# Attention of a hybrid encoder block on TensorE: score pairs in two row halves, V stationary with normalised probabilities moving in two column halves

## The reference

```python
h = rms_norm(x, mix_norm[l])
z = h @ w_in[l]                       # 1024 -> 2048: q | k | v | p, 512 columns each
a = neighborhood_attention(q, k, v, rpb[l])   # 8 heads of 64
m = multiscale_pool(p, w_pool[l], pool_scale[l])
x = x + jnp.concatenate([a, m], axis=-1) @ w_out[l]

# attention: tokens are a 4 x 64 grid, every query sees all 4 rows and 16 columns around its own
scores = q_r * Dh**-0.5 @ k_r.T + bias        # bias from rpb, by distance of rows and columns
scores = where(col_mask, scores, NEG_INF)
out    = softmax(scores) @ v_r

# pooling, group g of 128 channels, window w = 2, 4, 8, 16
mean = (csum[hi] - csum[lo]) / (hi - lo)      # lo = t - w//2, hi = lo + w, clipped
y    = (mean - p) @ w_pool[g] * scale
```

## Time and profile before

| | |
|---|---|
| median of 3 runs | 987.61 us (985.65 to 989.18) |
| span of the profiled execution | 983.4 us |
| TensorE busy | 958.7 us, 97% |
| VectorE busy | 552.3 us, 56% |
| ScalarE busy | 499.5 us, 51% |
| mean DMA rate | 178 GB/s |

### The profile page before, as it was taken

The page is one execution under the profiler, slowest core; times in us unless marked ns, Lnnn a source line. Parts: engine busy times, 40 slices in busy tenths (PEclk is TensorE's granted clock), DMA queues, the critical chain, the costliest instruction groups (busy, mean ns, idle before and its releaser), DMA issues.

```text
span 983.4 us, 13937 instructions
## 1 busy us (share of the span) xinstructions
PE 958.7 (97%) x4390; PEld 780.2 (79%) x4390; DVE 552.3 (56%) x865; ACT 499.5 (51%) x812; POOL 45.1 (5%) x86
## 2 busy tenths in 40 slices
PE   5989999999999999999989999999999999999996
PEld 4878888877788888888878888888868888888885
DVE  4556555467545665554466556564665565465644
ACT  4555455455625654544375545454664365454542
POOL 0550000010001000000010000000100010000000
PEclk9999999999999999999999999999999999999999
DMA  8998646527223746465367555644542266556441
GB/s 285 234 244 284 211 171 212 173 87 250 93 86 129 244 147 210 167 213 171 129 208 254 193 191 171 209 160 143 171 172 86 86 209 199 190 170 213 145 156 43
DMA packets 123269, 174.75 MB, mean 178 GB/s; under 512 B 8240, under 2 KB 99552, under 8 KB 122976
## 3 DMA queue, kind: packets, MB, share of 16 engines
q1 hardware_dynamic: 117328, 165.17, 50.1%
q0 software_dynamic: 2848, 6.38, 3.0%
q10 hardware_dynamic: 3056, 2.75, 0.8%
HBM read 173.14 MB, written 4.19 MB: 180 GB/s over the span
## 4 chain that ended last, share of the span: by engine, by line
issue 92%; POOL 4%; DMA 2%; PE 1%; ACT 0%; ACTq 0%; DVE 0%; POOLq 0%; DVEq 0%; SPq 0%
POOL bias_scratch L364 3%; POOL rstd L337 1%; DMA bias_scratch<-in_rpb_dram 1%; DMA w_raw<-in_ffn_w_up_dram 1%; POOL mean_eps L334 0%; PE ps L868 0%; POOL rstd_scaled L340 0%; PE ps L869 0%; ACT w_hi L416 0%; PE ps L918 0%; ACT L416 0%; POOL bias L371 0%; DVE normed L850 0%; DVEq L95 0%; ACT xt_hi L431 0%
## 5 line engine op out<-in xcount | busy, mean ns | idle before, releaser
L631 DVE SCALAR_TENSOR_TENSOR w_lo<-w_raw,gain,w_hi 128x512 fp32r<-128x512 f32 x416 | 285.4, 746 | 104.3 <-ACT w_hi L416 103.7
L860 PE MATMUL ps<-w_hi,xt_hi 128*128 128x512 f32 x848 | 338.3, 399 | 2.9 <-DVE w_lo L631 2.8
L861 PE MATMUL ps<-w_lo,xt_hi 128*128 128x512 f32 x848 | 330.4, 390 | 0.0
L863 PE MATMUL ps<-w_hi,xt_lo 128*128 128x512 f32 x848 | 326.2, 391 | 0.0
L416 ACT ACTIVATE w_hi<-w_raw,gain 128x512 fp32r<-128x512 f32 x416 | 265.7, 713 | 99.7 <-PE ps L863 78.2
L623 DVE TENSOR_TENSOR w_lo<-w_raw,w_hi 128x1024 fp32r<-128x1024 f32 x104 | 122.7, 1222 | 121.2 <-ACT w_hi L410 121.1
L860 PEld LDWEIGHTS ps<-w_hi,xt_hi 128*128 128x128 f32 x848 | 159.3, 188 | 39.1 <-DVE w_lo L631 4.7
L863 PEld LDWEIGHTS ps<-w_hi,xt_lo 128*128 128x128 f32 x848 | 159.2, 188 | 34.2
L861 PEld LDWEIGHTS ps<-w_lo,xt_hi 128*128 128x128 f32 x848 | 159.6, 188 | 30.4
L410 ACT ACTIVATE w_hi<-w_raw 128x1024 fp32r<-128x1024 f32 x104 | 104.4, 1052 | 105.0 <-PE ps L863 104.3
L860 PE MATMUL ps<-w_hi,gt_hi 128*128 128x512 f32 x352 | 140.0, 398 | 0.0
(11 more groups left out here) (82 smaller groups left out, 468.3 us busy)
## 6 DMA issues: line engine op xcount, KB each, us to landing
w_raw<-in_ffn_w_gate_dram SPq DMA_DIRECT2D x88, 512.0 KB, 4.0
w_raw<-in_ffn_w_up_dram SPq DMA_DIRECT2D x88, 512.0 KB, 5.1
w_raw<-in_ffn_w_down_dram SPq DMA_DIRECT2D x88, 512.0 KB, 4.0
w_raw<-in_w_in_dram SPq DMA_DIRECT2D x32, 512.0 KB, 4.7
w_raw<-in_w_out_dram SPq DMA_DIRECT2D x16, 512.0 KB, 5.2
bias_scratch<-in_rpb_dram POOLq DMA_DIRECT2D x32, 96.0 KB, 6.7
bias<-bias_scratch POOLq DMA_DIRECT2D x2, 1536.0 KB, 8.0
pool_m<-in_pool_matrix_dram ACTq DMA_DIRECT2D x1, 1024.0 KB, 6.5
```

Source lines behind the costliest of these rows:

```text
L631: nc.vector.scalar_tensor_tensor(w_lo[slot][:, part], w_raw[slot][:, part], g, w_hi[slot][:, part].bitcast(F32), ALU.mult, ALU.subtract).t ...
L860: nc.tensor.matmul(o, hi, wh, start=start, stop=False)
L861: nc.tensor.matmul(o, hi, wl, start=False, stop=False)
L863: last = nc.tensor.matmul(o, lo, wh, start=False, stop=stop)
```

## The change

- **Scores**: `pair_scores` takes two heads at once and alternates between them, the even head in rows 0 to 63 of the array, the odd one in rows 64 to 127. It waits until both heads of the pair before have been read. The places in `after` are thinned out to four pairs.
- **Normalisation**: VectorE's new `normalise` divides the probabilities of a head by their row sum before they are transposed: one reciprocal of two values, two multiplies of 128x256. `transpose_probs` waits for `normalised_ready` and no longer for `probs_ready`. The multiply of the outputs by the inverse sum is gone, and so is the reciprocal of all sums.
- **V times probabilities**: `pair_v` makes V stationary (128 rows x 64 columns) and moves the 256 columns of the transposed probabilities. The even head's output goes to PSUM partitions 0 to 63, the odd head's to 64 to 127. The result comes out with channels on partitions, so the transposes of the outputs are gone, and ScalarE and VectorE make `xt_hi` and `xt_lo` straight from banks 0 and 1.
- **Pool differences**: for the second tile of tokens (k = 1) only the columns from 120 (`POOL_FROM`) on are computed, as the window reaches no further back than 8 tokens. The others are zero in the matrix.
- **Order**: VectorE's queue has the eight `normalise` between its other pieces, and the output projection takes its first half for both row tiles in one go.

```diff
-            def head_scores(layer, h):
-                if h >= 2:
-                    pe.wait_ge(biased_ready, layer * N_HEADS + (h - 1))
-                rows = slice((h % 2) * HEAD_DIM, (h % 2 + 1) * HEAD_DIM)
-                for t in range(TT):
-                    last = nc.tensor.matmul(ps[:, 4 + h % 2, t * SEQ:(t + 1) * SEQ],
-                                            q_t[rows, h // 2, t, :], k_t[rows, h // 2, :, :],
-                                            start=True, stop=True)
-                last.then_inc(scores_ready, 1)
+            def pair_scores(layer, pair):
+                if pair >= 1:
+                    pe.wait_ge(biased_ready, layer * N_HEADS + 2 * pair)
+                for t in range(TT):
+                    for e in range(2):
+                        rows = slice(e * HEAD_DIM, (e + 1) * HEAD_DIM)
+                        last = nc.tensor.matmul(ps[:, 4 + e, t * SEQ:(t + 1) * SEQ],
+                                                q_t[rows, pair, t, :], k_t[rows, pair, :, :],
+                                                start=True, stop=True)
+                        if t == TT - 1:
+                            last.then_inc(scores_ready, 1)
...
             def transpose_probs(layer, h):
-                pe.wait_ge(probs_ready, layer * N_HEADS + (h + 1))
+                pe.wait_ge(normalised_ready, layer * N_HEADS + (h + 1))
...
-            def probs_v(layer, h):
-                wait_probs_t_stored(layer, h)
-                for t in range(TT):
-                    for k in range(TT):
+            def pair_v(layer, pair):
+                wait_probs_t_stored(layer, 2 * pair)
+                wait_probs_t_stored(layer, 2 * pair + 1)
+                cols = slice((pair % 2) * SEQ, (pair % 2 + 1) * SEQ)
+                for k in range(TT):
+                    for e in range(2):
+                        h = 2 * pair + e
                         last = nc.tensor.matmul(
-                            ps[:, t, h * HEAD_DIM:(h + 1) * HEAD_DIM],
-                            scores[:, h, k, t * P:(t + 1) * P],
+                            ps[e * HEAD_DIM:(e + 1) * HEAD_DIM, pair // 2, cols],
                             z[:, k, 3, h * HEAD_DIM:(h + 1) * HEAD_DIM],
+                            scores[:, h, k, :],
                             start=(k == 0), stop=(k == TT - 1))
                 last.then_inc(pv_ready, 1)
...
                     for k in range(TT):
+                        first = POOL_FROM * k
                         last = nc.tensor.matmul(
-                            ps[:, 4 + j, (g % 2) * SEQ:(g % 2 + 1) * SEQ],
-                            z[:, k, 2, g * P:(g + 1) * P], pool_m[:, k, g, :],
+                            ps[:, 4 + j, (g % 2) * SEQ + first:(g % 2 + 1) * SEQ],
+                            z[:, k, 2, g * P:(g + 1) * P], pool_m[:, k, g, first:],
                             start=(k == 0), stop=(k == TT - 1))
...
-                project_z(layer, 2, 1, after={1: lambda: s(1), 3: lambda: s(2),
-                                              5: lambda: (s(3), t(0)), 7: lambda: (s(4), t(1))})
-                project_z(layer, 3, 0, after={1: lambda: (s(5), t(2)), 3: lambda: (s(6), t(3)),
-                                              5: lambda: (s(7), t(4)), 7: lambda: t(5)})
+                project_z(layer, 2, 1, after={3: lambda: s(1), 5: lambda: t(0),
+                                              7: lambda: (s(2), t(1))})
+                project_z(layer, 3, 0, after={1: lambda: t(2), 3: lambda: (s(3), t(3)),
+                                              5: lambda: t(4), 7: lambda: t(5)})
...
+            def normalise(layer, h):
+                dve.wait_ge(probs_ready, layer * N_HEADS + (h + 1))
+                nc.vector.reciprocal(inv_sum[:, h, :], row_sum[:, h, :]).then_inc(inv_ready, 1)
+                dve.wait_ge(inv_ready, layer * N_HEADS + (h + 1))
+                for t in range(TT):
+                    done = nc.vector.tensor_scalar(scores[:, h, t, :], scores[:, h, t, :],
+                                                   inv_sum[:, h, t:t + 1], None, ALU.mult)
+                done.then_inc(normalised_ready, 1)
...
                 add_bias(layer, 1)
                 mix_unit(layer, 7, halves=(0,))
+                normalise(layer, 0)
+                normalise(layer, 1)
                 add_bias(layer, 2)
+                add_bias(layer, 3)
                 mix_unit(layer, 7, halves=(1,))
-                add_bias(layer, 3)
+                normalise(layer, 2)
+                store_probs_t(layer, 1)
                 add_bias(layer, 4)
-                store_probs_t(layer, 1)
+                normalise(layer, 3)
                 add_bias(layer, 5)
                 mix_unit(layer, 8)
+                normalise(layer, 4)
+                store_probs_t(layer, 3)
+                normalise(layer, 5)
                 add_bias(layer, 6)
-                store_probs_t(layer, 3)
                 add_bias(layer, 7)
                 store_kv(layer, 3, 0)
+                normalise(layer, 6)
                 store_probs_t(layer, 5)
+                normalise(layer, 7)
                 store_diffs(layer, 0)
```

More of the change, by code:

```diff
@@ L35 @@
 N_GROUPS = len(POOL_WINDOWS)
+POOL_FROM = 128 - max(POOL_WINDOWS) // 2
 D_FF = 2816
@@ L211, in trunk @@
         inv_ready = sem("inv_ready")
[L212 to L213 removed]
+        normalised_ready = sem("normalised_ready")
         heads_t_hi_ready = sem("heads_t_hi_ready")
@@ L529, in exps @@
                         scores[:, h, t, :], scores[:, h, t, :], ACT.Exp,
-                        bias=neg_max[:, h, t:t + 1], accum_out=row_sum[:, t, h:h + 1])
+                        bias=neg_max[:, h, t:t + 1], accum_out=row_sum[:, h, t:t + 1])
                 done.then_inc(probs_ready, 1)
@@ L579, in mix_stage @@
                 mix_unit(layer, 10)
-                for t in range(TT):
-                    act.wait_ge(heads_t_ready, layer * 2 + (t + 1))
-                    nc.scalar.activation(xt_hi[:, t, 0:4, :], ps[:, 6 + t, :], ACT.Copy
-                                         ).then_inc(heads_t_hi_ready, 1)
+                for b in range(2):
+                    act.wait_ge(pv_ready, layer * 4 + (2 * b + 2))
+                    nc.scalar.activation(
+                        xt_hi[:, :, 2 * b:2 * b + 2, :],
+                        ps[:, b, :].rearrange("p (g t q) -> p t g q", g=2, t=TT), ACT.Copy
+                    ).then_inc(heads_t_hi_ready, 1)
                 mix_unit(layer, 11)
@@ L808, in mix_stage @@
                         ALU.mult, ALU.subtract).then_inc(pooled_lo_ready, 1)
-                dve.wait_ge(inv_ready, layer + 1)
-                dve.wait_ge(pv_ready, layer * N_HEADS + N_HEADS)
-                for t in range(TT):
+                mix_unit(layer, 10)
+                for b in range(2):
+                    dve.wait_ge(heads_t_hi_ready, layer * 2 + (b + 1))
                     nc.vector.tensor_tensor(
[L813 to L822, removed]
+                        xt_lo[:, :, 2 * b:2 * b + 2, :],
+                        ps[:, b, :].rearrange("p (g t q) -> p t g q", g=2, t=TT),
+                        xt_hi[:, :, 2 * b:2 * b + 2, :].bitcast(F32), ALU.subtract
                     ).then_inc(heads_t_lo_ready, 1)
@@ L1122, in heads_k, with s @@
                     transpose_heads(layer, 1, h)
-                def s(h):
-                    if h == 0:
+                def s(pair):
+                    if pair == 0:
                         pe.wait_ge(k_t_stored, layer * 2 + 2)
-                    head_scores(layer, h)
+                    pair_scores(layer, pair)
                 def t(h):
@@ L1145, in mix_stage @@
                 pe.wait_ge(z_kv_stored, layer * 4 + 4)
[L1146 to L1147 removed]
+                for pair in range(N_HEADS // 2):
+                    pair_v(layer, pair)
                 pe.wait_ge(pooled_lo_ready, layer * N_GROUPS + N_GROUPS)
[L1150 to L1152 removed]
                 for t in range(TT):
[L1155 to L1163 removed]
+                    out_tile(layer, t, 8, 0, t == 0, start=True)
+                    last = out_tile(layer, t, 8, 1, t == 0)
+                    if t == 1:
+                        last.then_inc(w_out_used, 1)
+                    out_tile(layer, t, 9, 0, t == 0)
+                    last = out_tile(layer, t, 9, 1, t == 0)
+                    if t == 1:
+                        last.then_inc(w_out_used, 1)
                 for t in range(TT):
[L1165 removed]
                     for j in (10, 11):
+                        if t == 0:
+                            pe.wait_ge(heads_t_lo_ready, layer * 2 + (j - 9))
                         for k in range(2):
```

24 lines of the change are left out of this document (2 added, 22 removed).

## The result

The changed kernel takes 976.7 us (median of 4 runs, 975.76 to 980.33) against 986.63 us for the kernel before (4 runs, 985.23 to 989.18). The ratio is 0.9896, with a 95% interval of 0.987 to 0.9923: faster by about 1%. The forecast was 977.2. The profiled executions have spans of 983.4 and 974.3 us.

A forecast was written before the change was run, and what follows sets the result against it. TensorE's queue was taken as the path in the mixing stages. Per layer 4.2 + 3.0 + 0.9 + 0.8 - 3.7 = 5.2 us, for two 10.4: 983.4 - 10.4 + 4.2 = 977.2 us; forecast 975 to 981, overall range 973 to 987.

The forecast's parts named there:

- five lengths: Scores on TensorE: a pair's eight records take 0.41 + 5 x 0.2135 = 1.47 us, gaining 4.2 us per layer.
- the lower bound given: Scores on TensorE: four record lengths for a pair, 1.26 us; the kernel would then take 976 us.
- seventeen: V times probabilities on TensorE: 17 lengths + 0.41 = 4.04 us in alternating halves, gaining 3.0 us per layer.
- The rival by which the loads of V are left open: V times probabilities: each load waits until the array is free, 32 x 0.36 = 11.5 us; 992 us, chance 0.04.
- Transposes of the outputs and pool differences: TensorE, smaller parts: eight output transposes go, 0.87 us; narrower second-tile pool differences gain 0.8 us, per layer.
- Normalise: VectorE's queue: reciprocal and two multiplies take 0.64 us per head (0.24 + 2 x 0.20), bounds 0.54 and 0.90.
- Waits: TensorE waits at transposes 0, scores 4/5, scores 6/7, transposes 4 and transposes 6: 3.7 us per layer, paid in full.
- the same walk: Stepping three engine queues in order from 240.84 to find TensorE's waits; reproduced the kernel before within 0.2 us.
- One form only: Scores and V times probabilities: halves overlap in columns only (979.8 us) or rows only (983.6 us); chance 0.16.
- no overlap: Scores and V times probabilities: halves do not run at once; 986.2 us, 989 with the multiply at 0.42; chance 0.10.
- a price for each change of half: TensorE: each change of half costs 0.20 us like a change of form, 27 per layer; 996 us; chance 0.12.
- VectorE takes the gain: VectorE's queue: normalise above its upper end or copies queue worse, overlap intact; waits of 7 us, 984 us; chance 0.07.

The follow-up runs named there:

- the blocked order: Changed kernel with the two loops exchanged in pair_scores and pair_v: both matmuls of the even head, then both of the odd head; 976.07 us (1 run).
- one column half: Changed kernel with V times probabilities writing both heads of a pair through columns 0 to 63 of the array; 983.15 us (1 run).
- unit 8 moved: Changed kernel with only unit 8 moved in VectorE's queue, from before normalise 4 to behind normalise 6; 968.42 us, again 969.97 us.
- the early part reordered: Changed kernel with unit 8 behind normalise 6, normalise 0 and 1 ahead of unit 7, add_bias in pairs as early as their scores; 968.39 us, again 967.6 us.

## Why the prediction was right

The mechanism was the forecast one: the halves overlap, and VectorE's queue takes a part of the gain back, most of it at transposes 4. That the time came out only 0.5 us from the forecast is luck in part. Three terms of the sum were off and cancelled, and the medians themselves move by as much.

- **Scores.** The gain is 4.9 us for each layer, not 4.2. The step that failed is that an odd head's record could run only beside the even head's second, in program order, which gave five lengths. A pair takes four (1.26 us, the lower bound given). Two records of one half do follow each other, as assumed (2.12), but the halves don't wait for each other's turn, as the blocked order shows. The page TensorE: Matmul & The Clock Gate of the Trainium skill says, in its Part 3 on packing small matmuls, that matmuls start and end in program order. In the blocked order here the odd head's first record starts with the even head's first, although all four records of the even head stand ahead of it, and the measurement decides.
- **V times probabilities.** 3.81 instead of 4.04: sixteen lengths and the change of form, not seventeen. The gain is 3.3, not 3.0, since the piece before also costs 7.15 when it is read to the second record behind it, as the scores were, and not 7.07. The rival by which the loads of V are left open (11.5 us) is refuted by this figure, and by 7.26 in one column half. The changes into and out of the column halves cost what was taken from the row halves, 3.81 - 16 x 0.2125 = 0.41.
- **Transposes of the outputs and pool differences.** No record of the first is left, 0.87 as priced. A pool difference takes 270.25 - 0.23 - 268.69 = 1.33 instead of 1.72, so 0.8 for each layer, as priced.

```profile
268.69 1.49 PE L1097 MATMUL ps<-pool_m,z 128*128 128x256 f32 x8
269.93 0.48 PE L867 MATMUL ps<-w_hi,xt_hi 128*128 128x512 f32 x1
270.25 0.39 PE L868 MATMUL ps<-w_lo,xt_hi 128*128 128x512 f32 x1
```

- **Normalise.** 0.73 us of VectorE's queue (261.29 to 262.02), not 0.64, within the bounds. The reciprocal of two is 0.16, a multiply 0.35 long, and the next start comes 0.27 behind its own, against 0.29 and 0.20. A multiply of 2 elements (`neg_max`) takes 0.17, so the 254 elements more cost 0.18, or 0.72 ns each. Passes with two inputs in SBUF take 0.95 for 768 elements and 1.22 for 1024, 1.05 ns for each. So this multiply is the quicker of the two for each element. The page VectorE: DVE Perf Modes of the Trainium skill names, in "The perf-mode tier table", a doubled rate for a multiply by a scalar in fp32 in SBUF, and the trace doesn't speak against it; no run here has the same multiply at two lengths, so the rate stays open.
- **Waits.** All five came where they were forecast, in the same order of size for the two long ones: 2.6 and 1.0 against 2.1 and 0.8, and 0.6, 0.35 and 0.3 against 0.3, 0.4 and 0.1. The total is 4.8, not 3.7. Both errors above feed into it: shorter pairs bring TensorE to the transposes earlier (with pairs of 2.12 the wait at transposes 4 was 0.9 shorter), and a longer normalise holds VectorE. With the measured 1.26, 3.81 and 0.73 put in, so after the fact, the same walk gives the 4.8. It then foretold, before they ran, how the stretches of six other kernels would differ, within 0.25 us.
- **The sum.** For each layer 4.9 + 3.3 + 0.9 + 0.8 - 4.8 = 5.1, against 5.2 forecast; the stretch gives 42.32 - 38.10 + 0.87 = 5.09. Twice that is 10.2, where the medians show 9.9. That the spans differ by only 9.1 is because the changed kernel's profiled execution came to the first scores 1.15 us later, at 241.99 instead of 240.84, by work that isn't part of the change.
- **The rivals.** One form only, no overlap, and a price for each change of half are all refuted: with both heads in one half the pieces grow to 2.12 and 7.26, and the changed kernel has neither. "VectorE takes the gain" was half true: its queue takes 4.8 of the 9.9 us that the change frees on TensorE in each layer, but by order and not by load: with unit 8 moved, 1.3 us are left of it, and with the early part reordered too, nothing.

## What to carry to other kernels

When TensorE's queue is the path and a piece of it is made shorter, walk the queues of the engines that feed it with the new due times: an item that nobody needs soon (here a weight split 20 us ahead of its use) becomes a wait as soon as something urgent stands behind it. Here it was worth about as much as the change itself to put the queue into the order of need. And judge small steps by a stretch between two marks in the trace, which repeated within 0.1 us, when the device time spreads by several microseconds. Look at the granted clock too, since a fall of it lengthened the stretch by 0.6 us in two kernels.

## What the hardware showed that was not expected

- Two row halves, or two column halves, run fully at once in fp32: eight records in the time of four (1.26 against 2.12 us with both heads in one half), 32 in that of 16 (3.81 against 7.26). The order in the program, alternating or two by two, made almost no difference (1.28 and 3.86).
- Behind a wait of 2.35 us, TensorE's granted clock stayed at 1.00 in both profiled executions of the changed kernel, in both layers, and fell in those of the blocked order and of V in one column half, in both layers: there it averaged 0.76 to 0.81 over two windows of 4 us in layer 0. Such a fall cost 0.6 us of the stretch. The kernels in which that wait is gone, or shorter than 1.5 us, had none there.
